# Narrow norms, an opening in blocks of tokens, and ada slabs moved into merge, in a fused two-block transformer kernel

## The chip, the cores and the metric

The kernel runs on 1 core of one Trainium2 chip. The metric is device time in microseconds (us); the time before is 2602.92 us, the median of 3 runs (2602.31 to 2603.13). The engines are PE (TensorE), DVE (VectorE), ACT (ScalarE), POOL (GpSimd) and SP (SyncE, which issues DMAs).

## The reference, cut to what matters

A block with three branches (forgetting attention, an S5 recurrence, attention over a memory) and a norm behind it, then two layers of a second block whose norms are modulated by a vector `c`:

```python
def rms(x, g):
    return x * rsqrt(mean(x * x, -1) + 1e-6) * g          # x: 512 tokens x 1024

def first_block(x, mem, ...):
    h = rms(x, g_norm)
    q, k, v, fl, gf, u, gs, qm, gm, gl = split_cols(h @ w_in)
    y_fox = forgetting_attention(q, k, v, log_sigmoid(fl + b_forget)) * silu(gf)
    y_s5 = ...     # s5_ssm(u, ...), gelu, glu with w_glu, * silu(gs)
    y_mem = ...    # attention to mem, * silu(gm)
    gates = sigmoid(gl + b_merge)                          # three gates of 1024
    merged = sum(gates[b] * (y[b] @ w_proj[b]) for b in range(3))
    return rms(x + merged @ w_out, g_final)

def second_block(x, c, ...):
    for l in range(2):
        sh1, sc1, gt1, sh2, sc2, gt2 = split(silu(c) @ w_ada[l] + b_ada[l], 6)
        h = rms(x, g_mix[l]) * (1 + sc1) + sh1
        mixed = ...    # h @ w_in_2[l], two attentions with rope and norms, gates
        x = x + gt1 * (mixed @ w_out_2[l])
        h2 = rms(x, g_mlp[l]) * (1 + sc2) + sh2
        x = x + gt2 * (square(relu(h2 @ w_ff1[l])) @ w_ff2[l])
    return x
```

All in float32.

## The kernel before, in words

**Layout.** x and h stand transposed in SBUF, as `xT` and `hT`: 8 tiles (k = 0 to 7) of 128 channels by 512 tokens. `hT` is a pair, a rounded high part (`hT_high`, type fp32r) and the rest (`hT_low`), and a product is three matmuls: high x high, low x high, high x low. A tile of output (128 columns of weights by 512 tokens) takes 8 x 3 = 24 matmuls (L433 in `tiles_stage`, L525 in `Stream`).

**Weights.** They come in slabs of 1 MB (256 columns by 1024 rows) through a ring of 3 slots (`SLOTS`). `plan_slabs` writes their order down; `load_weights` (SP) issues them in that order, and slab i waits until slab i-3 is given up (by the split, by a reduction or by PE). POOL splits a slab into a high and a low part in halves of 128 columns (L226, then L228), into 4 buffers for halves. The projections of merge (`w_proj_*`) are used without a split.

**Ada slabs.** `silu(c) @ w_ada` has one row only. Its 48 slabs stand between the others, one at a time: ACT scales a slab in place (L332, 8 operations), DVE reduces it (L345), PE adds over the partitions (L358, `ada_sum`), and DVE takes the result (L368, `ada_take`). In a stage these steps hang on the tiles: a slab whose last neighbour is tile n is handled from tile n-2 on. PE's sum of a slab waits until the last one was taken.

**A norm** (`rms_stage`). Squares on ACT (L612), sums over channels with a matrix of ones on PE (L627, the result on all partitions), a root on ACT (L614, 128x512), a reciprocal on DVE (L646, 128x512), and then per k: normed tile on DVE (L651), high part on ACT (L619), low part on DVE (L639 or L641). L631 are products without use that keep PE going. The first product that follows waits for each k (`arriving`): its tile takes one k at a time as `hT` arrives, and the next tile comes after it. With `summed` the squares were added up on DVE before (`add_square`, L584 and L585), behind each residual.

**The order of the stages.** `load_stage` loads the constants, x and small vectors, turns them on PE (L430) and copies them out on DVE. Then `s5_stages`: nine loads of parameters on ACT's queue (L997 to L1006), the first norm, the products u, gs, q and k, and in parallel a long DVE chain on the S5 parameters, which begins with their turn on PE (L1149) and has the sines on ACT (L1213, L1214) in its middle. `merge_stage` goes through four groups of columns (mp), in each three pairs (b) of a gate slab and a projection slab; a pair makes two tiles, 2 x (24 + 12) or 2 x (24 + 8) matmuls; ACT takes the gate (L1702), DVE multiplies and adds (L1708 to L1715). The last product of the first block, `out` (L433, taken by L1773), has four slabs with one ada slab each. Then come the norm `g_final` and, in `layer`, the gains (L1994, L1995), nine loads for rope and its gains on ACT's queue (L2000, L2006), the mixer's norm and qkv (L1858, tiles of 128 tokens by 256 columns). Behind attention: the residual (L2138), the mlp norm, and the mlp with relu (L2167) and the square (L2179 to L2181), where ada slabs stand again in layer 0.

## Time and profile before

| what | value |
|---|---|
| median of 3 runs | 2602.92 us |
| profiled execution | 2601.7 us, its span 2599.7 us |
| mean granted PE clock | 0.964 |
| PE busy | 2384.8 us, 92% of the span |
| DVE busy | 1454.2 us, 56% |
| POOL busy | 1126.4 us, 43% |
| ACT busy | 597.2 us, 23% |
| HBM read | 257.87 MB |

The span runs from the first to the last instruction of the profiled execution; all times of events are counted from its start. Busy time is the time with an instruction in execution. An instruction's bracket at the end of a row of the timeline, as [0.73 <-DVE normed L651], says how long the engine stood idle before it and which engine's work, which tile and line, ended that. Chain rows give the start, the duration, the engine and the line of a stretch on the chain that ended last, and the number of its instructions. The granted clock (PEclk) is a share of full speed, 1.00 for 2.4 GHz and 0.50 for 1.2 GHz.

### The profile page before, as it was taken

What the parts mean: (1) busy time and instruction counts of PE and PEld (TensorE: products, weight loads), DVE (VectorE), ACT (ScalarE), POOL (GpSimd) and SP (SyncE); (2) the same over time, 40 slices, a digit from 0 to 9 for tenths busy, and PEclk for the clock granted to TensorE, in tenths of its full rate; (3) what the DMA queues carried; (4) which work ended last, traced back from release to release, by engine and by line L of the source; (5) the groups of instructions that cost most, each with busy time, mean ns of one, the idle gap of its engine ahead of it and who ended that gap; (6) DMA issues with size and microseconds to landing.
All of it is one profiled execution on the core that took longest, in us unless ns stands there. A gap on an engine that the chain in (4) does not pass through costs nothing.

```text
span 2599.7 us, 30892 instructions
## 1 busy us (share of the span) xinstructions
PE 2384.8 (92%) x12709; PEld 1889.6 (73%) x12709; DVE 1454.2 (56%) x1756; ACT 597.2 (23%) x1212; POOL 1126.4 (43%) x672
## 2 busy tenths in 40 slices
PE   5798868799999969999998999998999999899998
PEld 3677835677666639977756888886997766688887
DVE  3799444424333667455458857747645537764341
ACT  2133325313222221134402334201114430100000
POOL 3543223143333525642124666663662305466663
PEclk8899978899999989999999999998999999999999
DMA  5334660341444432221032665533231104233321
GB/s 163 114 77 111 182 235 1 122 146 61 133 146 148 157 96 99 97 78 48 18 107 72 202 192 177 178 109 103 89 98 61 34 17 146 65 98 98 97 97 49
DMA packets 274280, 280.87 MB, mean 108 GB/s; under 512 B 29580, under 2 KB 256080, under 8 KB 274012
## 3 DMA queue, kind: packets, MB, share of 16 engines
q1 hardware_dynamic: 242012, 243.97, 29.6%
q10 hardware_dynamic: 32128, 34.92, 4.4%
q8 instruction: 101, 1.65, 0.3%
q14 instruction: 39, 0.32, 0.0%
HBM read 257.87 MB, written 17.85 MB: 106 GB/s over the span
## 4 chain that ended last, share of the span: by engine, by line
PE 68%; DVE 5%; ACT 1%; issue 1%; ACTq 0%; DVEq 0%
PE ps L433 43%; PE ps L1858 11%; PE ps L525 6%; PE ps L757 2%; PE ps L800 2%; PE ps L776 1%; DVE ps L864 1%; DVE normed L651 1%; DVE hT_low L641 1%; PE ps L786 1%; DVE root L646 1%; PE ps L627 1%; PE ps L1954 1%; PE ps L358 0%; DVE squares_summed L585 0%
## 5 line engine op out<-in xcount | busy, mean ns | idle before, releaser
L226 POOL TENSOR_SCALAR ring_high<-ring 128x1024 fp32r<-128x1024 f32 x302 | 335.1, 1110 | 1347.7 <-DMA ring<-in_w_in_dram 360.9
L228 POOL TENSOR_TENSOR ring_low<-ring,ring_high 128x1024 fp32r<-128x1024 f32 x302 | 762.2, 2524 | 25.2
L433 PE MATMUL ps<-hT_high,ring_high 128*128 128x512 f32 x816 | 329.1, 403 | 19.1 <-DVE hT_low L641 5.8
L433 PE MATMUL ps<-hT_low,ring_high 128*128 128x512 f32 x816 | 319.3, 391 | 0.0
L433 PE MATMUL ps<-hT_high,ring_low 128*128 128x512 f32 x816 | 319.2, 391 | 0.0
L345 DVE TENSOR_REDUCE ada_acc<-ring 128x256 f32<-128x2048 f32 x48 | 188.8, 3934 | 111.4 <-ACT ring L332 111.1
L1858 PE MATMUL ps<-ring_high,hT_high 128*128 128x256 f32 x768 | 221.8, 289 | 10.4 <-DVE hT_low L641 10.4
L1858 PE MATMUL ps<-ring_high,hT_low 128*128 128x256 f32 x768 | 219.6, 286 | 0.0
L1858 PE MATMUL ps<-ring_low,hT_high 128*128 128x256 f32 x768 | 219.5, 286 | 0.0
L332 ACT ACTIVATE ring<-ring,c_act 128x256 f32<-128x256 f32 x384 | 158.5, 498 | 186.2 <-DMA ring<-in_w_ada_dram 186.1
L433 PE MATMUL ps<-hidden_high,ring_high 128*128 128x512 f32 x512 | 200.0, 391 | 0.0
L525 PE MATMUL ps<-hT_high,ring_high 128*128 128x512 f32 x456 | 191.5, 420 | 9.2 <-ACT staged L1042 3.7
L433 PE MATMUL ps<-hidden_high,ring_low 128*128 128x512 f32 x512 | 199.3, 389 | 0.0
L433 PE MATMUL ps<-hidden_low,ring_high 128*128 128x512 f32 x512 | 199.2, 389 | 0.0
L433 PEld LDWEIGHTS ps<-hT_high,ring_high 128*128 128x128 f32 x816 | 154.3, 189 | 59.8 <-DVE hT_low L641 11.7
L525 PE MATMUL ps<-hT_low,ring_high 128*128 128x512 f32 x456 | 180.9, 397 | 0.0
L525 PE MATMUL ps<-hT_high,ring_low 128*128 128x512 f32 x456 | 180.8, 396 | 0.0
L433 PEld LDWEIGHTS ps<-hT_low,ring_high 128*128 128x128 f32 x816 | 154.3, 189 | 32.9 <-issue 2.9
L433 PEld LDWEIGHTS ps<-hT_high,ring_low 128*128 128x128 f32 x816 | 154.0, 189 | 32.6
L2138 DVE SCALAR_TENSOR_TENSOR xT<-ps,ada,xT 128x512 f32<-128x512 f32 x64 | 47.9, 750 | 220.9 <-PE ps L433 220.9
L1858 PEld LDWEIGHTS ps<-ring_high,hT_high 128*128 128x128 f32 x768 | 149.6, 195 | 14.7 <-DVE hT_low L641 11.1
L1858 PEld LDWEIGHTS ps<-ring_high,hT_low 128*128 128x128 f32 x768 | 149.9, 195 | 0.0
(341 smaller groups left out, 4164.1 us busy)
## 6 DMA issues: line engine op xcount, KB each, us to landing
ring<-in_w_in_dram SPq DMA_DIRECT2D x75, 1024.0 KB, 5.3
ring<-in_w_ff_dram SPq DMA_DIRECT2D x64, 1024.0 KB, 5.5
ring<-in_w_ada_dram SPq DMA_DIRECT2D x48, 1024.0 KB, 7.3
ring<-in_w_out_dram SPq DMA_DIRECT2D x12, 1024.0 KB, 6.6
scratch_x<-xT ACTq DMA_DIRECT2D x3, 2048.0 KB, 7.5
xT<-scratch_x ACTq DMA_DIRECT2D x3, 2048.0 KB, 8.6
ring<-in_w_mem_kv_dram SPq DMA_DIRECT2D x4, 1024.0 KB, 5.5
ring<-in_w_branch_a_dram SPq DMA_DIRECT2D x8, 512.0 KB, 6.1
```

Source lines behind the costliest of these rows:

```text
L226: nc.gpsimd.tensor_scalar(hi, raw, 1.0, 1.0, ALU.mult, ALU.mult).then_inc(hi_done.sem, 1)
L228: nc.gpsimd.tensor_tensor(lo, raw, hi.bitcast(F32), ALU.subtract).then_inc(lo_done.sem, 1)
L332: ins = K.nc.scalar.activation(w[:, k, :], w[:, k, :], ACT.Copy, scale=K.c_act[:, k:k + 1])
L345: K.nc.vector.tensor_reduce(K.ada_acc[:, n % 2, :], K.slot(slab).rearrange("p k n -> p n k"), AX_X, ALU.add).then_inc(K.sig("ada_scaled"). ...
L433: ins = nc.tensor.matmul(out[0:rows, bank, cols[0]:cols[1]], lhsT, rhs, start=start, stop=stop)
L525: ins = K.nc.tensor.matmul(out, lhsT, rhs, start=start, stop=stop)
L627: nc.tensor.matmul(K.ps[:, 0, 0:n], K.ones, K.sums[:, 0:n] if summed else sq[:, k % 2, 0:n], start=(k == 0), stop=(k == KS - 1)).then_inc( ...
L641: x = v.scalar_tensor_tensor(dst[1][:, k, 0:n], tmp[:, k % 2, 0:n], shift[:, k:k + 1], h, ALU.add, ALU.subtract)
L757: ins = nc.tensor.matmul(s_view(i, u, w)[:, c:c + n], lhsT, rhs, start=True, stop=st["diagonal"] is None or c + n < w)
L800: ins = nc.tensor.matmul(st["place"](o_view(j), u), st["values"](u, b), turned[j % T_BUFS][:, u, b * P:(b + 1) * P], start=(b == 0), stop= ...
L1858: ins = nc.tensor.matmul(out, lhsT, rhs, start=start, stop=stop)
L2138: return v.scalar_tensor_tensor(K.xT[:, m, :], ps[:, 0, :], gate[:, m:m + 1], K.xT[:, m, :], ALU.mult, ALU.add)
```

## The change

- **Opening** (`load_stage`). Slab 0 is loaded in front of x, and x in four blocks of 128 tokens, each with its own semaphore. ACT squares each block along its free axis with a sum of it (4 operations of 128x1024), one root and one reciprocal of 128x4 follow, and the rstd of the 512 tokens is put on all partitions by a product of ones with four diagonal matrices (128x512, `diag`). The transposes of x go block by block, the copies out of PSUM are shared by DVE and ACT, and the first norm is a part of this stage. The silu of `c` comes behind it. The S5 parameters are loaded by SP, in front of slab 3.
- **Norms** (`norm_stage`). The sums over channels are made narrow: each block of 128 tokens is the stationary side and a column of ones moves, so a sum is 128x1 and all four are 128x4. Root and reciprocal work on 128x4; the diagonals and one product spread the result. The last square is not added on DVE but summed by PE on its own. A small root in front loads ACT's table early. Behind `out`, one stage makes both norms (`twice`): from the sums of the squares of x and of x times `g_final` it has both factors, makes `hT` at once, and writes the normed `xT` afterwards. The squares behind `out` move from DVE to ACT (`out_squares`), the sums stay on DVE, one tile later.
- **First products.** Where a product waits for arriving tiles, its first two tiles (at qkv token tiles 0 and 2, then 1 and 3, of the first slab) are interleaved k by k.
- **Ada slabs.** Each of the four groups of merge has one more ada slab, behind the first gate slab; `out` has none.
- **Rope loads.** Those of layer 0 are issued ahead of `out`, those of layer 1 behind the mlp norm of layer 0.

```diff
+        if i == 0:
+            continue
...
             add(f"merge{mp}{b}g", w, dm, O_GL + D * b, D, part=mp)
+            if b == 0:
+                ada(0)
             add(f"merge{mp}{b}p", T[pw][0], (0, rows), 0, D, False, part=mp)
             ada(0)
-    add_ada("out", T["w_out"][0], dm, 0, D, 0)
+    add("out", T["w_out"][0], dm, 0, D)
...
+            if arriving is not None:
+                first = 2
+                size = len(tiles[0])
+                per = 1 if tiles[0][0][5][1] is None else 3
+                for j in range(0, size, per):
+                    pe.wait_ge(arriving[0].sem, arriving[1] + max(j // per + 1, arriving[3]))
+                    for n in range(2):
+                        for x in range(j, j + per):
+                            ins = product(n, x)
+                        if j + per == size:
+                            ins.then_inc(made.sem, 1)
...
+            if self.arriving is not None and n < 2:
+                k, x = divmod(self.fed, 6)
+                n, j = x // 3, 3 * k + x % 3
+                if x == 0:
+                    pe.wait_ge(self.arriving[0].sem, self.arriving[1] + k + 1)
...
+    if n == 0:
         return K.nc.vector.tensor_tensor(K.sums, x, x, ALU.mult)
-    K.link(e, "dve_step", K.nc.vector.tensor_tensor(sq, x, x, ALU.mult))
+    ins = K.nc.vector.tensor_tensor(sq, x, x, ALU.mult)
+    if n == KD - 1:
+        return ins
+    K.link(e, "dve_step", ins)
     return K.nc.vector.tensor_tensor(K.sums, K.sums, sq, ALU.add)
 
...
+def norm_stage(K, src, gain, dst, shift, sums, last, twice=None):
...
+            nc.scalar.activation(nar[:, 6, 0:1], K.eps[:, 0:1], ACT.Sqrt)
...
+            def turn(bank, x, last):
+                for t in range(TT):
+                    ins = nc.tensor.matmul(ps[:, bank + t, 0:1], x[:, t * P:(t + 1) * P], K.ones[:, 0:1],
+                                           start=not last, stop=last)
+                return ins
...
+            if twice is not None:
+                squared, summed = twice[0]
+                pe.wait_ge(tiles.sem, tiles.total - 1)
+                pe.wait_ge(summed.sem, summed.total)
+                turn(2, twice[3], False)
+                warm(2)
+                pe.wait_ge(squared.sem, squared.total - 1)
+                turn(2, twice[4], True).then_inc(turned.sem, 1)
+                for t in range(TT):
+                    x = slice(t * P, (t + 1) * P)
+                    nc.tensor.matmul(ps[:, 6, t:t + 1], sums[:, x], K.ones[:, 0:1], start=True, stop=False)
+                    if t == 0:
+                        pe.wait_ge(squared.sem, squared.total)
+                    ins = nc.tensor.matmul(ps[:, 6, t:t + 1], last[:, x], K.ones[:, 0:1], start=False, stop=True)
+                ins.then_inc(turned.sem, 1)
+                pe.wait_ge(tiles.sem, tiles.total)
+                warm(2)
+            else:
+                pe.wait_ge(tiles.sem, tiles.total - 1)
+                turn(2, sums, False)
+                warm(1)
+                pe.wait_ge(tiles.sem, tiles.total)
+                turn(2, last, True).then_inc(turned.sem, 1)
+                warm(1)
+            pe.wait_ge(diagonal.sem, d0 + 1)
+            nc.tensor.matmul(ps[:, 7, :], K.ones, diag[:, 0], start=True, stop=True).then_inc(spread.sem, 1)
+            if twice is not None:
+                nc.tensor.matmul(ps[:, 6, :], K.ones, diag[:, 1], start=True, stop=True).then_inc(spread.sem, 1)
+                warm(1)
+            else:
+                warm(3)
+        @block.scalar
+        def _(e):
+            if twice is not None:
+                e.wait_ge(turned.sem, t0 + 1)
+                nc.scalar.activation(nar[:, 0, :], ps[:, 2:6, 0], ACT.Sqrt, bias=K.eps[:, 0:1], scale=1.0 / D
+                                     ).then_inc(root.sem, 1)
+                e.wait_ge(scaled.sem, s0 + 1)
+                nc.scalar.activation(nar[:, 3, :], nar[:, 2, :], ACT.Sqrt, bias=K.eps[:, 0:1], scale=1.0 / D
+                                     ).then_inc(root.sem, 1)
+            else:
+                e.wait_ge(turned.sem, t0 + 1)
+                nc.scalar.activation(nar[:, 3, :], ps[:, 2:6, 0], ACT.Sqrt, bias=K.eps[:, 0:1], scale=1.0 / D
+                                     ).then_inc(root.sem, 1)
...
+        @block.vector
+        def _(e):
+            step = lambda ins: K.link(e, "dve_step", ins)
+            def diagonals(j, x):
+                return v.tensor_tensor(diag[:, j], K.ident.unsqueeze(1).broadcast_to([P, TT, P]),
+                                       x.unsqueeze(2).broadcast_to([P, TT, P]), ALU.mult)
+            n = 0
+            e.wait_ge(root.sem, o0 + 1)
+            if twice is not None:
+                step(v.reciprocal(nar[:, 1, :], nar[:, 0, :]))
+                e.wait_ge(turned.sem, t0 + 2)
+                step(v.tensor_tensor(nar[:, 2, :], ps[:, 6, 0:TT], nar[:, 1, :], ALU.mult))
+                v.tensor_tensor(nar[:, 2, :], nar[:, 2, :], nar[:, 1, :], ALU.mult).then_inc(scaled.sem, 1)
+                diagonals(1, nar[:, 1, :])
+                e.wait_ge(root.sem, o0 + 2)
+                step(v.reciprocal(nar[:, 4, :], nar[:, 3, :]))
+                step(v.tensor_tensor(nar[:, 4, :], nar[:, 4, :], nar[:, 1, :], ALU.mult))
+                n = 1
+            else:
+                step(v.reciprocal(nar[:, 4, :], nar[:, 3, :]))
+            diagonals(0, nar[:, 4, :]).then_inc(diagonal.sem, 1)
+            def low_part(k):
+                e.wait_ge(high.sem, h0 + k + 1)
+                v.scalar_tensor_tensor(dst[1][:, k, :], tmp[:, k % 2, :], shift[:, k:k + 1], dst[0][:, k, :].bitcast(F32),
+                                       ALU.add, ALU.subtract).then_inc(low.sem, 1)
+            e.wait_ge(spread.sem, w0 + 1)
...
+    def load_parameters(sp):
...
+        sp.wait_ge(K.sig("x_turned").sem, KD)
+        sp.wait_ge(K.sig("x_squared").sem, TT)
+        sp.dma_start(lamn[:, 0, 0:P5], T["lam_re"][0]).then_inc(loaded.sem, 16)
...
+    K.sync_turns[K.first["u"] + SLOTS] = [load_parameters]
...
+            sp.dma_start(K.const[:, :], T["const_main"]).then_inc(cl.sem, 16)
+            sp.dma_start(K.slot(0), K.slabs[0][0][0]).then_inc(K.sig("slab_landed0").sem, 16)
+            for t in range(TT):
+                sp.dma_start(xn[:, t, :], T["x"][0, t * P:(t + 1) * P, :]).then_inc(xl[t].sem, 16)
...
+            pe.wait_ge(cl.sem, 16)
+            for t in range(TT):
+                pe.wait_ge(xl[t].sem, 16)
+                for n in range(KD):
+                    ins = nc.tensor.transpose(ps[:, n, t * P:(t + 1) * P], xn[:, t, n * P:(n + 1) * P], K.ident)
+                    if t == TT - 1:
+                        ins.then_inc(turned.sem, 1)
+            pe.wait_ge(ld.sem, 16 * (2 + len(vec)))
...
+            pe.wait_ge(diagonal.sem, 1)
+            nc.tensor.matmul(ps[:, 1, :], K.ones, diag[:, :, :], start=True, stop=True).then_inc(spread.sem, 1)
+            pe.wait_ge(by_dve.sem, 3)
+            for _ in range(3):
+                nc.tensor.matmul(ps[:, 2, 0:3 * P], K.ident, K.const[:, 0:3 * P], start=True, stop=True)
+        @block.scalar
+        def _(e):
+            e.wait_ge(eps.sem, 1)
+            nc.scalar.activation(nar[:, 6, 0:1], K.eps[:, 0:1], ACT.Sqrt)
+            for t in range(TT):
+                e.wait_ge(xl[t].sem, 16)
+                if t:
+                    e.wait_ge(squared.sem, t)
+                nc.scalar.activation(squares[:, :], xn[:, t, :], ACT.Square, accum_out=nar[:, 0, t:t + 1]
+                                     ).then_inc(squared.sem, 1)
+            e.wait_ge(squared.sem, TT)
+            nc.scalar.activation(nar[:, 3, :], nar[:, 0, :], ACT.Sqrt, bias=K.eps[:, 0:1], scale=1.0 / D
+                                 ).then_inc(root.sem, 1)
...
+            evict(0)
+            evict(1)
+            e.wait_ge(root.sem, 1)
+            K.link(e, "dve_step", v.reciprocal(nar[:, 4, :], nar[:, 3, :]))
+            v.tensor_tensor(diag[:, :, :], K.ident.unsqueeze(1).broadcast_to([P, TT, P]),
+                            nar[:, 4, :].unsqueeze(2).broadcast_to([P, TT, P]), ALU.mult).then_inc(diagonal.sem, 1)
+            evict(2)
+            evict(3)
+            e.wait_ge(by_dve.sem, 4)
+            e.wait_ge(cols.sem, 1)
+            e.wait_ge(spread.sem, 1)
...
+    rope_loads(K, T, 0)
...
+        if 2 <= n:
+            e.wait_ge(squared.sem, 2 * n)
+            for x in range(2):
+                a = square[:, 0, x, :] if n == 2 else sums[x]
+                ins = v.tensor_tensor(sums[x], a, square[:, (n - 1) % 2, x, :], ALU.add)
+            ins.then_inc(summed.sem, 1)
...
+    def out_squares(e, n):
+        e.wait_ge(added.sem, added0 + n + 1)
+        if n >= 2:
+            e.wait_ge(summed.sem, n - 1)
+        nc.scalar.activation(square[:, n % 2, 0, :], xq[:, n, :], ACT.Square).then_inc(squared.sem, 1)
+        nc.scalar.activation(square[:, n % 2, 1, :], xq[:, n, :], ACT.Square, scale=K.g_final[:, n:n + 1]
+                             ).then_inc(squared.sem, 1)
...
+                    order = [(t + u, 3 * k + x) for u in range(2) for k in range(KD) for t in (0, 2) for x in range(3)]
...
+            if l == 0:
+                K.link(e, "gains_ready", v.tensor_scalar(gains[:, 2, :], ada[:, 16:24], 0.5, None, ALU.mult))
+                v.tensor_tensor(gains[:, 3, :], gains[:, 0, :], K.g_final, ALU.mult).then_inc(ga.sem, 1)
+            else:
+                v.tensor_scalar(gains[:, 2, :], ada[:, 16:24], 0.5, None, ALU.mult).then_inc(ga.sem, 1)
...
+        arriving = norm_stage(K, xq, gains[:, 3, :], K.hT, ada[:, 0:8], sums[1], last[1],
+                              (squared, K.g_final, K.xT, sums[0], last[0]))
+    else:
+        K.close(gains=ga)
+        arriving = norm_stage(K, K.xT, gains[:, 0, :], K.hT, ada[:, 0:8], K.sums, K.square_last)
...
-    arriving = rms_stage(K, K.xT, SEQ, gains[:, 1, :], K.hT, shift=ada[:, 24:32], summed=True)
+    arriving = norm_stage(K, K.xT, gains[:, 1, :], K.hT, ada[:, 24:32], K.sums, K.square_last)
+    if l + 1 < LAYERS:
+        rope_loads(K, T, l + 1)
```

SP's loads in the second group of merge, before (`ring<-in_w_in` is a gate slab, `ring<-in_w_ada` an ada slab, in brackets what the slot waits for):

```order
L202 DMA ring<-in_w_in_dram 128x8x256 [waits half_split]
L202 DMA ring<-in_w_proj_fox_dram 128x6x256 [waits tile_made]
L202 DMA ring<-in_w_ada_dram 128x8x256 [waits ada_scaled]
L202 DMA ring<-in_w_in_dram 128x8x256 [waits half_split]
L202 DMA ring<-in_w_proj_s_dram 128x6x256 [waits tile_made]
```

and now:

```order
L204 DMA ring<-in_w_in_dram 128x8x256 [waits half_split]
L204 DMA ring<-in_w_ada_dram 128x8x256 [waits tile_made]
L204 DMA ring<-in_w_proj_fox_dram 128x6x256 [waits ada_scaled]
L204 DMA ring<-in_w_ada_dram 128x8x256 [waits half_split]
L204 DMA ring<-in_w_in_dram 128x8x256 [waits ada_scaled]
L204 DMA ring<-in_w_proj_s_dram 128x6x256 [waits tile_made]
```

An ada slab stands between the gate slab and the first projection slab, and the next gate slab waits for an ada slab's slot instead of a split.

ACT at the mlp norm of layer 0, before:

```order
L614 ACT_TABLE_LOAD [waits x_back,square_used,tile_made]
L614 ACTIVATE root_9849<-ps,eps 128x512 [waits tile_taken]
L619 ACTIVATE hT_high<-normed_9850,ada 128x512 [waits norm_scaled] x8
L79 UNCONDITIONAL_BRANCH
L2167 ACTIVATE relu_9928<-ps 128x512 [waits norm_high,tile_made,square_used,norm_low]
L332 ACTIVATE ring<-ring,c_act 128x256 [waits slab_landed2]
```

and now:

```order
L718 ACT_TABLE_LOAD
L718 ACTIVATE narrow<-eps 128x1
L79 UNCONDITIONAL_BRANCH
L778 ACTIVATE narrow<-ps,eps 128x4 [waits x_back,sums_turned,tile_taken,tile_made]
L784 ACTIVATE hT_high<-normed_9831,ada 128x512 [waits norm_scaled] x8
L79 UNCONDITIONAL_BRANCH
L2281 DMA rope_9916<-in_const_rope_dram 128x1024 [waits norm_low,norm_high,rstd_spread]
L2287 DMA gn_9917<-in_q_norm_a_dram 128x64
L2287 DMA gn_9917<-in_k_norm_a_dram 128x64
```

The table is loaded without a wait, root and sum are 128x4, and the nine loads for layer 1's rope (three of them shown) stand between the last high part and the first relu.

ACT in the opening, before, from the silu of `c` to the first squares:

```order
L1564 ACTIVATE c_act<-cols 128x8 [waits inputs_loaded]
L79 UNCONDITIONAL_BRANCH
L997 DMA lamn<-in_lam_re_dram 48x64 [waits c_activated,biases_halved]
L998 DMA lamn<-in_lam_re_dram 48x64
L999 DMA lamn<-in_lam_im_dram 48x64
```

and now, its first operations:

```order
L1749 ACT_TABLE_LOAD
L1749 ACTIVATE narrow<-eps 128x1 [waits eps_set]
L1754 ACTIVATE x_squares,narrow<-xn 128x1024 [waits x_loaded0]
L1754 ACTIVATE x_squares,narrow<-xn 128x1024 [waits x_squared,x_loaded1]
L1754 ACTIVATE x_squares,narrow<-xn 128x1024 [waits x_squared,x_loaded2]
L1754 ACTIVATE x_squares,narrow<-xn 128x1024 [waits x_squared,x_loaded3]
L1757 ACTIVATE narrow<-narrow,eps 128x4 [waits x_squared]
```

The squares wait for a block of x each and for nothing else; the loads of the parameters have left ACT's queue.

## Rows read from the trace of the kernel before

**Rows 1.** The page, part 4: chain that ended last, by engine.

```profile
PE 68%; DVE 5%; ACT 1%; issue 1%; ACTq 0%; DVEq 0%
```

**Rows 2.** Windows of the opening: busy time (count) by engine, PEclk, DMA share, GB/s.

```profile
7.00:8.00 1.00, 0.00 (x0) 0.00 (x0) 0.00 (x0) 0.00 (x0) 0.00 (x0) 1.00 1.03 401
```

**Rows 3.** Timeline of PE, opening: start us, us, line, operation, count [idle before <-releaser].

```profile
10.93 0.59 PE L430 MATMUL ps<-const,rows 100*128 100x100 f32 x2 [10.93 <-DMA b_forget_col<-in_b_forget_dram]
61.37 0.39 PE L1149 MATMUL ps<-const,lamn 48*128 48x48 f32 x3
```

**Rows 4.** Timeline, opening: POOL, then DVE.

```profile
17.84 2.36 POOL L228 TENSOR_TENSOR ring_low<-ring,ring_high 128x1024 fp32r<-128x1024 f32 x1
...
40.33 3.35 DVE L646 RECIPROCAL root<-root 128x512 f32<-128x512 f32 x1 [20.09 <-ACT root L614]
43.71 1.42 DVE L651 SCALAR_TENSOR_TENSOR normed<-xT,cols,root 128x512 f32<-128x512 f32 x2
```

**Rows 5.** Timeline of ACT, the sines of the S5 coefficients.

```profile
109.40 1.28 ACT L1213 ACT_TABLE_LOAD   x1
```

**Rows 6.** Merge: page part 6; ACT and DVE timelines; chain row of PE.

```profile
ring<-in_w_in_dram SPq DMA_DIRECT2D x75, 1024.0 KB, 5.3
...
651.21 0.69 ACT L1702 ACTIVATE merge_tmp<-ps,half_b_merge 128x512 f32<-128x512 f32 x1 [6.67 <-PE ps L433]
...
698.78 3.30 ACT L332 ACTIVATE ring<-ring,c_act 128x256 f32<-128x256 f32 x8 [6.95 <-DMA ring<-in_w_ada_dram]
...
644.57 3.79 DVE L345 TENSOR_REDUCE ada_acc<-ring 128x256 f32<-128x2048 f32 x1 [2.41 <-ACT ring L332]
...
714.27 0.15 DVE L368 TENSOR_TENSOR ada<-ps,cols 128x2 f32<-128x2 f32 x1
...
691.44 21.40 PE ps L433 x72
```

**Rows 7.** `out` and the norms behind it: chain rows, timelines, one window.

```profile
879.86 18.25 PE ps L433 x72
...
926.86 0.50 PE L358 MATMUL ps<-const,ada_acc 128*128 128x1 f32 x4
...
930.87 2.65 POOL L228 TENSOR_TENSOR ring_low<-ring,ring_high 128x1024 fp32r<-128x1024 f32 x1
...
917.51 0.69 DVE L585 TENSOR_TENSOR squares_summed<-squares_summed,square 128x512 f32<-128x512 f32 x1
...
962.49 1.41 DVE L651 SCALAR_TENSOR_TENSOR normed<-xT,gains,root 128x512 f32<-128x512 f32 x2
...
973.54 137.81 PE ps L1858 x1134
...
970.00:980.00 10.00, 8.48 (x47) 7.73 (x48) 9.77 (x32) 2.12 (x3) 0.00 (x0) 0.67 0.48 178
```

**Rows 8.** Mlp norm of layer 0: timelines; L627 by its source (ns, min/median/max); chain row.

```profile
947.71 0.45 ACTq L2006 DMA_DIRECT2D gn<-in_k_norm_b_dram  x1
...
1393.22 2.65 POOL L228 TENSOR_TENSOR ring_low<-ring,ring_high 128x1024 fp32r<-128x1024 f32 x1
...
1393.71 2.71 DVE L585 TENSOR_TENSOR squares_summed<-squares_summed,squared 128x512 f32<-128x512 f32 x1
...
L627 PE MATMUL ps<-squares_summed,const x8: 667/1061/1221, 931.5 to 2223.8; 128*128 128x512 f32 x8
...
1404.15 1.42 DVE L651 SCALAR_TENSOR_TENSOR normed<-xT,gains,root 128x512 f32<-128x512 f32 x2
...
1417.16 0.60 ACT L2167 ACTIVATE relu<-ps 128x512 f32<-128x512 f32 x1 [1.92 <-PE ps L433]
...
1435.84 11.02 PE ps L433 x48
```

**Rows 9.** Timeline of DVE, mixer norm of layer 1.

```profile
1777.52 0.24 DVE L1994 SCALAR_TENSOR_TENSOR gains<-ada,cols 128x8 f32<-128x8 f32 x2
...
1786.10 1.41 DVE L651 SCALAR_TENSOR_TENSOR normed<-xT,gains,root 128x512 f32<-128x512 f32 x2
```

More of the change, by code:

```diff
@@ L397, in tiles_stage @@
             ada.setdefault(max(n - 2, 0), []).append(K.ada_after[key])
+    for slabs in ada.values():
+        slabs.sort()
     if ada and dve is None:
@@ L438, in _ @@
                 ada_sum(K, pe, s)
-        if act is None and ada:
+        if act is None and (ada or also is not None):
             @block.scalar
@@ L443, in _ @@
                 for n in range(N):
+                    if also is not None:
+                        also(e, n)
                     for s in ada.get(n, []):
@@ L656, in _ @@
                 low_part(KD - 1)
[L658 to L659 removed]
+    ready.total += KD
+    used.total += KD
     root.total += 1
@@ L1503, in load_stage @@
     rows = R("rows", [P, 2, P], 24576)
-    ld = K.sig("inputs_loaded")
+    squares = R("x_squares", [P, D], 28672)
+    diag = R("diagonals0", [P, TT, P], 49152)
+    tmp = R("normed0", [P, 2, SEQ], 57344)
+    nar, dst = K.narrow, K.hT
+    ld, cl = K.sig("inputs_loaded"), K.sig("const_loaded")
+    xl = [K.sig(f"x_loaded{t}") for t in range(TT)]
     vec = [("g_norm", 8), ("g_mem_norm", 8), ("g_final", 8), ("b_merge", 24), ("s5_d", 6), ("b_glu", 6),
@@ L1553, in load_stage @@
+    ld.total += 16 * (2 + len(vec))
+    cl.total += 16
+    for g in (*xl, ):
+        g.total += 16
+    for g in (eps, root, diagonal, spread, rows_turned, cols):
+        g.total += 1
+    for g in (squared, by_dve, by_act):
+        g.total += 4
+    for g in (turned, scaled, high, low):
+        g.total += KD
+    K.close(loads=ld, tensor=spread, xdve=by_dve, xact=by_act, cols=cols)
+    arriving = (low, 0, dict(K.last), 1)
+    K.close(scalar=high, vector=low)
     ha, si = K.sig("biases_halved"), K.sig("c_activated")
@@ L2006, in _, with layer @@
                 e.dma_start(gn[:, i, :], a.broadcast_to([P, HD])).then_inc(rl.sem, 16)
-    ga.total += 1
-    K.close(vector=ga)
-    arriving = rms_stage(K, K.xT, SEQ, gains[:, 0, :], K.hT, shift=ada[:, 0:8], summed=l > 0)
+def layer(K, T, l):
+    nc, R = K.nc, K.region
+    v = nc.vector
+    gains = K.gains
+    ada = K.ada[:, l, :]
+    ga = K.sig("gains_ready")
+    rope, gn = K.rope
+    with K.stage() as block:
+        @block.vector
+        def _(e):
+            for i, (at, g) in enumerate(((8, K.g_mix[l]), (32, K.g_mlp[l]))):
+                v.scalar_tensor_tensor(gains[:, i, :], ada[:, at:at + 8], 1.0, g, ALU.add, ALU.mult)
+            if l == 0:
[3 more added lines that the diff above has]
+                v.tensor_scalar(gains[:, 2, :], ada[:, 16:24], 0.5, None, ALU.mult).then_inc(ga.sem, 1)
+    ga.total += 1
+    if l == 0:
+        K.close(vector=ga)
+        xq, squared, sums, last = K.outer
+        arriving = norm_stage(K, xq, gains[:, 3, :], K.hT, ada[:, 0:8], sums[1], last[1],
[3 more added lines that the diff above has]
+        arriving = norm_stage(K, K.xT, gains[:, 0, :], K.hT, ada[:, 0:8], K.sums, K.square_last)
     sx, xs = K.scratch_x.rearrange("(t p) n -> p t n", p=P), K.sig("x_spilled")
```

294 lines of the change are left out of this document (180 added, 114 removed).

## The prediction

> **What bounds the kernel now.** I read the chain that ended last first: TensorE (PE) holds 68% of it and VectorE 5% [rows 1]. PE is busy 92% of the span, so a cheaper operation elsewhere is worth nothing unless PE waits for it. The views by time come next, since such an average hides the places where PE stands. There are five: the opening; the change of norm after `out`; and the norm ahead of the mlp or the mixer three times more. The opening's first product of `hT` can't start before VectorE's L651 at 43.71 [rows 4], and the next piece of work, L1149, starts at 61.37 [rows 3]. After the last product of `out` (with its sums, 927.36) the first L651 of the mixer's norm is at 962.49 [rows 7], 35.1 us later. Last come the two stages into which the removed ada slabs move: the four groups of merge, where PE runs without a gap [rows 6], so that whatever arrives late there is paid in full.
>
> **The opening.** Before, nothing is computed until the last small vector has landed at 10.93 [rows 3], the squares stand on ScalarE (ACT) behind nine parameter DMAs, and a wide root and a wide reciprocal (3.35 us [rows 4]) follow. After, x comes in four blocks, each squared at once. DMA moves 401 GB/s in the window in which x ends [rows 2], so the 1 MB slab in front costs x 2.6 us at that rate; I take 3, since not every window reaches it, so the last block lands near 11.8 and the vectors near 13.9. Last square 12.9, narrow root 13.2, narrow reciprocal and diagonals (0.24 and 0.75 us by their nearest operations) 14.3; the vectors' transposes stand ahead of the spread on PE, so it runs 14.6 to 16; the copies out of PSUM end at 15.9. First normed tile 16.0 to 17.5; I take 16.8. From there to L1149 it was 17.66 us, of which 24 matmuls of 0.227 (5.45) were the second tile; it is now interleaved, so 6 matmuls (1.38) ride on each 1.39 us step, with 0.7 left at the end: 12.9. Slab 1 is split by POOL from about 16 to 23, and each of its L228 (2.36 [rows 4]) can hold a low-part subtraction that reads two SBUF tiles: two of them, 3.7. End: 33.4 instead of 61.4, 28.0 gained. The parameters, now on SP behind x, land by 31 at the latest, just in time. The VectorE chain of the S5 coefficients starts at L1149 and runs unbroken to the sines; there a table load of 1.28 stood in front of them [rows 5], and the order no longer has one: 1.3. **Opening: 29** (bounds 20, if the clock, the parameters or a slow first block eat 9; 32, if no subtraction meets a split).
>
> **Merge.** It takes four more ada slabs. First, in group 0 the gate slab of branch 1 must wait for the ring slot of an ada slab, free when its reduction ends at 648.36 [rows 6]: 5.3 us to land and 3.5 for its first half's split give 657.2, where its tile was due at 651.2: the wait is about 5.7. Second, in the three later groups the projection slab now stands behind an ada slab on SP. Before, it was the ada slab that stood behind, and it was there at 698.78, 7.34 behind the group's first product at 691.44 [rows 6]; the projection's products come 24 x 0.227 = 5.45 behind it: 1.9 each, 5.7. (The Trainium skill, DMA: Bandwidth & Descriptors, Queues, rings and completion order, has the descriptors of one queue start in order; a reader may say that they overlap and the projection lands sooner. By the rule the wait is 1.9; by free overlap it is 0.) Third, two ada sums now stand behind one another, and the second waits for the first to be taken: from the tile's end at 712.84 to the take's end at 714.42 plus a hand-over, 1.75, three times, and 2.6 at the tile with two VectorE operations: 7.85. **Merge: -19.3** (0 if none of the three arises; -25 if each wait also lets the clock fall). **`out`** loses its four sums with their gaps, 0.5 each [rows 7]: **+2.1**.
>
> **Norm after `out`.** The first norm of all of x and the second are one now. Count from PE's end: the residual 1.2, two squares on ACT 1.3, narrow turns on PE (a 128x1 product of fp32 with its loads costs what the four of L358 show, 0.5 for two) 2 to 2.3, two narrow roots, two reciprocals and three products some 2, the diagonals 0.75, the spread 1.35 (two passes of 0.667 at full clock, 1.2 each at the worst [rows 8]). That is 8.8; POOL splits until about 6 us behind PE's end [rows 7], which can hold the first diagonals, so I take 10.5 for the first normed tile, against 35.1: 24.6. The first qkv slab then interleaves two token tiles: 24 matmuls of 0.12 (137.81 over 1134 [rows 7]) go under the steps, 2.8; and the half-clock stretch behind the norm (granted 0.67 over 970 to 980 [rows 7]) is entered with less to do: 2.2. **24.6 + 5.0 = 29.6.** Bounds 22 (wide, blocked by POOL) and 31.
>
> **Mlp norm, layer 0.** The chain was square, sum, one wide product, table, wide root, wide reciprocal. The sum (2.71 under POOL's 2.65 [rows 8], 0.69 without it [rows 7]) and the wide steps go; what is left of it that reads two SBUF tiles is the diagonals, and they wait for POOL to end at 1395.87. Then 0.75, spread 1.35, hand-overs 0.25: first normed at 1398.2 instead of 1404.15. (The Trainium skill, GPSIMD Engine Reference, Specifications, says that GpSimd and VectorE contend where VectorE has two SBUF inputs; the trace agrees, 2.71 against 0.69. By the rule the diagonals wait for the split, without it they would start at 1395.) The last low part is at 1410.1. But nine rope DMAs are now queued on ACT ahead of the first relu: 9 x 0.48 = 4.3 [rows 8], so the relu is at 1414.45, not 1411.5; it was 1417.16, 2.7 later. Behind the relu hangs a fixed chain to tile 4: ada scale, reduction, slab load, split, 18.7 us (1417.16 to 1435.84 [rows 8]). PE sits idle through 10 us of it and starts again at the lower clock; the restart in `out` cost 1.9 (18.25 for 72 products that take 16.35 at 0.227 [rows 7]). **+1** (bounds -2 and 9, if the chain let tile 4 start as early as the norm).
>
> **Mixer norm, layer 1.** POOL's split holds the gains until 1777.5 [rows 9]; gains 0.4, reciprocal 0.24, diagonals 0.75, spread 1.35: 1780.0 against 1786.10, 6.1. Its half-clock stretch is the longer one, interleave and clock together 6.2. **+12.3** (8 to 14). **Mlp norm, layer 1.** As layer 0 to its first normed tile, 5.95 earlier, but with no rope DMA and no ada behind it. The second tile's 5.45 goes under the steps and 0.6 of it comes back at the end, 4.85: **+10.8** (6 to 11).
>
> **Sum.** 29 - 19.3 + 2.1 + 29.6 + 1 + 12.3 + 10.8 = 65.5. The profiled execution took 2601.7 us (span 2599.7), 1.2 below the median 2602.92; 2601.7 - 65.5 = 2536.2, and as a median about **2537**.
>
> **Rivals.** *The merge costs don't arise*: the projection and ada land side by side, or the gate's slab gets its slot early. For it, the DMA engines are idle ahead of each group; against it, 7.34 for the same bytes. All 19.3 come back: 2518. *The opening keeps only 20*: the parameters arrive late, or the clock falls in the wait behind the spread. For it, VectorE's chain, which ends the S5 coefficients, also waits for DMA; against it, SP can issue them from about 13.5 on, and that chain asks for them 20 us later. The 9 are lost: 2546. *The lock*: the narrow operations meet POOL or the lower clock in all four norms, the diagonals' 2.65 twice and a spread of 2.4; 3 each, 12 in all: 2549. For it, 2.71 on the sums of both layers; against it, one split is over in 2.7 and POOL has nothing more to do until tile 0 is through. *The other side, slower*: PE now stands between many short products and falls to its lower clock (window 970 to 980 was 0.67) and stays there through qkv. Each of its 1134 matmuls would cost 0.12 more; the change's gain is gone from some 540 matmuls on, and one whole stage gives 2537 + 138 = 2675. Against it, the 1134 matmuls behind the norm of before took 0.12 on average, though the first of them ran in that state.
>
> **How the numbers follow.** Forecast 0.55, merge for nothing 0.13, opening 20 0.13, the lock 0.15, slower 0.03, and 0.01 that the edits cancel. A change of 0.2%, 5 us, is what a measurement of this kernel can tell. All but the last two end below 2597: faster 0.96, same 0.01, slower 0.03. The range 2514 to 2562 holds the forecast with the bounds of its terms and the first three rivals' centres; the tails of these, the slower case and sums of two rivals leave some 2 in 10 out.
>
> **What would show it.** In the profile after: the first normed tile near 16.8 and L1149's place near 33.4; PE waiting for a projection slab in three merge groups and for the gate's split in the first; `out` without sums; the first normed tile behind `out` at PE's end + 10.5; relu of layer 0 behind the rope DMAs and PE idle before tile 4; and the product after each norm two tiles wide. I am wrong if the time is above 2562, most likely through the clock, or below 2514, if merge hides its slabs.

## The result, and the profile after

The changed kernel takes 2572.8 us (median of 4 runs, 2570.01 to 2575.04), the kernel before in the same and the earlier runs 2602.61 (2593.82 to 2603.13). The ratio is 0.9884, 95% interval 0.987 to 0.9897: some 30 us faster, where 65 were forecast. The profiled execution has a span of 2572.3 us against 2599.7, so 27.4 us are to be found in the traces.

| stretch (its end, before and after) | forecast | measured | with the placement mended (e1) |
|---|---|---|---|
| opening, to merge's first product (627.72, 600.26) | 29 | 27.5 | 29.3 |
| merge (876.12, 882.17) | -19.3 | -33.5 | -31.5 |
| `out` (927.36, 932.48) | 2.1 | 0.9 | 2.2 |
| norm behind `out` and qkv (1111.35, 1092.94) | 29.6 | 23.5 | 21.5 |
| attention and `out` of layer 0 (1392.04, 1374.78) | 0 | -1.1 | -1.3 |
| mlp norm and mlp, layer 0 (1773.10, 1759.71) | 1 | -3.9 | 2.8 |
| mixer norm to `out`, layer 1 (2218.32, 2196.20) | 12.3 | 8.7 | 10.1 |
| mlp norm to the end, layer 1 | 10.8 | 5.3 | 10.4 |
| sum | 65.5 | 27.4 | 43.5 |

The last column is the profiled execution of the first experiment.

**The opening** answers to [rows 3, 4]. From the timeline after, PE, VectorE and POOL (start, duration, line, operation, in brackets the idle time before and what ended it):

```profile
15.51 1.10 PE L1741 MATMUL ps<-diagonals,const 128*128 128x512 f32 x2 [0.37 <-DVE diagonals L1782]
33.94 0.38 PE L1329 MATMUL ps<-const,lamn 48*128 48x48 f32 x3
...
14.66 0.69 DVE L1782 TENSOR_TENSOR diagonals<-const,narrow 128x512 f32<-128x512 f32 x1
16.75 1.41 DVE L1800 SCALAR_TENSOR_TENSOR normed<-xT,cols,ps 128x512 f32<-128x512 f32 x2 [0.20 <-PE ps L1741]
18.20 2.83 DVE L1792 TENSOR_TENSOR hT_low<-normed,hT_high 128x512 fp32r<-128x512 f32 x1
23.17 2.08 DVE L1792 TENSOR_TENSOR hT_low<-normed,hT_high 128x512 fp32r<-128x512 f32 x1
...
18.13 2.34 POOL L230 TENSOR_TENSOR ring_low<-ring,ring_high 128x1024 fp32r<-128x1024 f32 x1
22.01 2.69 POOL L230 TENSOR_TENSOR ring_low<-ring,ring_high 128x1024 fp32r<-128x1024 f32 x1
```

The first normed tile comes at 16.75 (forecast 16.8) and the turn of the S5 parameters, L1329, at 33.94 (forecast 33.4, before 61.37), 27.4 us earlier. Of the eight low parts two ran under POOL's split, 2.83 and 2.08 instead of 0.68, as reckoned.

**Merge**, chain after, first group, the second group's first tiles (start, duration, engine, line, number):

```profile
600.26 13.52 PE ps L431 x36
614.57 3.21 ACT ring L336 x8
617.80 3.79 DVE ada_acc L349
621.61 5.35 DMA ring<-in_w_in_dram
628.16 2.35 POOL ring_low L230
630.55 13.75 PE ps L431 x36
...
650.88 12.14 PE ps L431 x36
663.36 17.91 PE ps L431 x64
681.70 7.21 DMA ring<-in_w_proj_fox_dram
688.95 16.07 PE ps L431 x48
...
707.31 22.98 PE ps L431 x72
```

and what PE waited for in merge (in total, times, longest):

```profile
PE ps L362 <- DVE ada L372: 9.4, 4, 5.3
PE ps L431 <- POOL ring_low L230: 6.1, 1, 6.1
PE ps L431 <- DMA ring<-in_w_proj_fox_dram: 6.0, 3, 2.5
```

The mechanisms are those of the forecast. In the first group the second gate slab is loaded when the ada slab is reduced (621.61), lands and is split, and PE waits 6.1 us (5.7 forecast). In each later group PE waits for the projection slab, 6.0 in three. The sums of ada waited 9.4 (7.85 forecast), of which 5.3 in the first group where 2.6 was put down: there VectorE reduces the next ada slab ahead of the tile's two operations and the take:

```profile
644.74 3.62 DVE L349 TENSOR_REDUCE ada_acc<-ring 128x256 f32<-128x2048 f32 x1 [18.82 <-PE ps L362]
```

So PE stands 21.6 us in merge, where it stood for nothing before, and the forecast had 19.3. The other 12 us of the 33.5 are not waits. The mean granted clock of the stage is 0.95 instead of 0.99: after, beside a stretch at the start that both have, it is 0.50 for 10.2 us from 626.4, for 6.8 from 646.9 and for 3.4 from 708.4 and from 776.6. So 36 products take 13.75 and 12.14 us in the first group and 72 take 22.98 and 22.99 in the second and third, where 72 took 21.40 before, 10.7 for 36 [rows 6]: 7.7 us. The 48 products right behind the projection slab lose nothing: 24 of them are the projection's (429 ns each, before and after), and 21.40 less 24 x 0.227 is 15.95, against 16.07. The four more sums take 0.6 to 1.0 each, 2.7. (The Trainium skill, DMA: Bandwidth & Descriptors, Queues, rings and completion order, has descriptors of one queue start in order; the trace agrees: ada slab, projection slab and ada slab, issued at 681.28, 681.70 and 682.33, land in this order at 686.66, 688.90 and 691.81.)

**The norm behind `out`** [rows 7], after:

```profile
932.51 2.13 DVE L2046 TENSOR_TENSOR squares_summed<-squares_summed,square 128x512 f32<-128x512 f32 x2 [2.49 <-PE ps L431]
934.57 1.08 DVE L2049 SCALAR_TENSOR_TENSOR x_by_residue<-ps,xT 128x512 f32<-128x512 f32 x1
943.54 0.69 DVE L798 TENSOR_TENSOR diagonals<-const,narrow 128x512 f32<-128x512 f32 x1
946.67 1.41 DVE L826 SCALAR_TENSOR_TENSOR normed<-x_by_residue,gains,ps 128x512 f32<-128x512 f32 x2 [2.43 <-PE ps L760]
...
937.05 1.69 PE L727 MATMUL ps<-const,square 128*128 128x1 f32 x8
938.60 0.56 PE L745 MATMUL ps<-const,squares_summed 128*128 128x1 f32 x2
939.03 0.57 PE L748 MATMUL ps<-const,square 128*128 128x1 f32 x2
944.71 1.91 PE L760 MATMUL ps<-diagonals,const 128*128 128x512 f32 x2
```

PE's last product ends at 932.48; the first normed tile follows after 14.2 us, not 10.5 (before 35.1). The last residual (L2049) stands behind two sums (L2046, 2.13; POOL splits beside them, until 936.87). The twelve narrow products behind the squares (L727 four; L745 and L748 four each, of which one pair of each is shown; two passes a product) take 5.1 us from 937.05, where 2 to 2.3 was forecast: the granted clock is 0.50 from 937.0 to 947.2. POOL's split was over when the diagonals came, and they took 0.69.

That it is the clock, a second execution of the same norm shows. In the profiled one of e12 below, the clock stayed at 1.00 until the products were done:

```profile
937.57 0.95 PE L727 MATMUL ps<-const,square 128*128 128x1 f32 x8
938.38 0.36 PE L745 MATMUL ps<-const,squares_summed 128*128 128x1 f32 x2
...
939.94 0.36 PE L748 MATMUL ps<-const,square 128*128 128x1 f32 x2
```

The twelve take 2.7 us there, from 937.57 to 940.30, and the first normed tile comes 11.6 us behind the last product of `out`. In e1, e7 and e9 the clock fell earlier, 2 to 3 us behind that product; there the products without use in front of the narrow ones ran at the lower clock too and held them up, and the tile came after 16.1 to 16.3. So this norm varies by 4.7 us between executions of the same instructions, with the moment at which the clock falls; what sets that moment no run shows.

**The mlps.** The chain rows of the last one, before and after:

```profile
2241.48 344.59 PE ps L433 x1518
```

```profile
2204.35 353.97 PE ps L431 x1536
```

344.59 over 1518 is 227.0 ns a product, 353.97 over 1536 is 230.4. PE waits for nothing in either and its granted clock is 1.00 in both. That was in no part of the forecast. Product by product, in the stages at full clock, the gap from one start to the next is 226.8 ns before everywhere in the mlp; after, it is 226.8 where `hT` is the moving operand and 233.3 where `hidden` is, and the same 233.3 in the three `out` products (`merged`, `mixed`).

### The profile page after: what moved, and what is told of

The parts are those of the page before. It is cut to its first block, busy times and chain, and to the rows that moved or that the text cites. A ratio compares the mean times of both kernels' runs of the same rounds, so it can differ in the third digit from the quotient of the medians.

```text
span 2572.3 us, 30947 instructions
## 1 busy us (share of the span) xinstructions
PE 2382.6 (93%) x12717; PEld 1890.9 (74%) x12717; DVE 1422.9 (55%) x1754; ACT 600.9 (23%) x1231; POOL 1133.7 (44%) x672
## 4 chain that ended last, share of the span: by engine, by line
PE 68%; DVE 4%; ACT 1%; DMA 1%; issue 1%; POOL 1%; ACTq 0%; DVEq 0%; SPq 0%; POOLq 0%
PE ps L431 44%; PE ps L2148 10%; PE ps L552 6%; PE ps L940 2%; PE ps L983 2%; PE ps L959 1%; DVE ps L1047 1%; DMA ring<-in_w_proj_fox_dram 1%; PE ps L969 1%; DVE normed L826 1%; DVE hT_low L819 1%; PE ps L2244 1%; PE ps L362 0%; DVE ada_acc L349 0%; ACT probs_b L1002 0%
## 5 line engine op out<-in xcount | busy, mean ns | idle before, releaser
L228 POOL TENSOR_SCALAR ring_high<-ring 128x1024 fp32r<-128x1024 f32 x302 | 344.2, 1140 | 1310.8 <-DMA ring<-in_w_in_dram 382.2
L431 PE MATMUL ps<-hT_high,ring_low 128*128 128x512 f32 x816 | 323.7, 397 | 0.0
L431 PE MATMUL ps<-hT_low,ring_high 128*128 128x512 f32 x816 | 323.6, 397 | 0.0
L552 PE MATMUL ps<-hT_high,ring_low 128*128 128x512 f32 x456 | 182.4, 400 | 0.0
L552 PE MATMUL ps<-hT_low,ring_high 128*128 128x512 f32 x456 | 182.4, 400 | 0.0
```

Of the source, the lines that this page charges most:

```text
L228: nc.gpsimd.tensor_scalar(hi, raw, 1.0, 1.0, ALU.mult, ALU.mult).then_inc(hi_done.sem, 1)
L431: return nc.tensor.matmul(out[0:rows, bank, cols[0]:cols[1]], lhsT, rhs, start=start, stop=stop)
L552: ins = K.nc.tensor.matmul(out, lhsT, rhs, start=start, stop=stop)
```

## The experiments

**e1 to e3, e12: where the operands lie.** The change makes `gains` larger (by 32 bytes a partition) and adds `narrow` (112 bytes, which take 128, since each tensor starts at a multiple of 32). These small tensors stand in front of `xT`, `hT` and the ring, which thereby move by 160 bytes and start 32 bytes off a multiple of 64, while the regions (`hidden`, `merged`, `mixed`) are rounded up to one. e1 puts them back:

```diff
+    K.pad = nc.alloc_sbuf_tensor("pad", [P, 8], F32)
     K.rowsum = nc.alloc_sbuf_tensor("rowsum", [P, 4, 2], F32)
```

> The changed kernel with 32 more bytes per partition allocated in front of xT, so that xT, hT and the weight ring start at a multiple of 64 bytes, as they do in the kernel before; in the changed one they start 32 bytes off, while hidden and merged start at a multiple of 64. Theory A (where the operands of a product lie sets its pace): the 512-wide products of out and of the second half of the mlp, at 233.3 ns each in the changed kernel and 226.7 in the one before, are all at 226.7 again; some 2100 of them by 6.67 ns is 14 us, so 2558 to 2560. Theory B (the pace belongs to the execution or to the instruction stream): 2572 as before, and the blocks of 233.3 ns stay.

Measured 2557.07 us (2551.18 to 2566.07), ratio to before 0.9824 (0.9801 to 0.9848). Chain row of the last mlp:

```profile
2193.48 348.77 PE ps L431 x1536
```

348.77 over 1536: 227.1 ns. Theory A holds. e2 is the kernel before with the same line:

> The kernel before with the same 32 bytes, which here move xT, hT and the ring 32 bytes off a multiple of 64 and leave hidden and merged on one. Theory A: slower by some 14 us (2603 to 2617) with blocks of 233.3 ns in the products of hidden and merged. Theory B: the time of before within 2 us.

Measured 2615.1 us against 2603.12, ratio 1.0046 (1.0029 to 1.0063), so 12 us slower, 14 forecast; 233.3 ns in all products of `hidden`, `mixed` and `merged`. e3 leaves out the rounding, so that both operands are 32 bytes off:

```diff
-    base = (nc.sbuf_base + 63) // 64 * 64
+    base = nc.sbuf_base
```

> The changed kernel with xT, hT and ring 32 bytes off as it has them, and the regions (hidden, merged, normed and others) not rounded up to 64 bytes, so that these lie 32 bytes off too. Theory A1 (what counts is that the moving and the stationary operand lie alike): all products at 226.7, 2558 to 2560. Theory A2 (what counts is each operand alone against 64 bytes): nothing is gained, 2572, or more if the elementwise work suffers too.

Measured 2558.76 us, ratio 0.9827 (0.9812 to 0.9841): as good as e1. e12 is e1 with the regions moved:

```diff
-    base = (nc.sbuf_base + 63) // 64 * 64
+    base = (nc.sbuf_base + 63) // 64 * 64 + 32
```

> The aligned kernel with xT, hT and ring at a multiple of 64 bytes and the regions (hidden, merged and the others) 32 bytes off, the mirror of the changed kernel. Theory A1 (moving and stationary operand must lie alike): products of hidden and merged at 233.3 ns again, 12 to 16 us slower than the aligned kernel. Theory A2 (it is the stationary operand's 32 bytes that cost, and only where hT does not lie the same way): stays at 226.7 and at the aligned time.

Measured 2573.48 us in one run. The last mlp of e3 and of e12:

```profile
2194.12 348.74 PE ps L431 x1536
```

```profile
2203.52 353.98 PE ps L431 x1536
```

With the kernel before, these are all four combinations, and the two where both lie alike are the fast ones. So neither operand's own place sets the pace but the difference of the two: 226.8 ns where moving and stationary operand lie alike against 64 bytes, 233.3 where they differ by 32. 2112 products (192 of `merged`, 384 of `mixed`, 1536 of `hidden`) times 6.5 ns are 13.7 us, and the medians differ by 15.7 between e1 and the changed kernel, whose runs (2551 to 2566, 2570 to 2575) leave room for that. Only offsets of 0 and 32 bytes were run.

**e4: the ada slabs of merge back in `out`.**

```diff
-            if b == 0:
-                ada(0)
...
-    add("out", T["w_out"][0], dm, 0, D)
+    add_ada("out", T["w_out"][0], dm, 0, D, 0)
```

> The aligned kernel with the four ada slabs of merge back in out, as before. If merge lost 33 us by them (from the traces: its first group 17.6 longer, the next three 5.6, 6.3 and 3.6) and out gained 1, this is 30 us faster than the aligned kernel, less what of the 33 was the slower pace: 2528 to 2534. If the loss in merge has another cause (the shifted opening, the pace), it is within 5 us of the aligned one.

Measured 2547.46 us (ratio 0.9782, 0.9766 to 0.9799), 10 below e1 instead of 30. Merge was right: 598.52 to 844.95, 246.4 us, against 248.4 before and 279.9 in e1. The gain went to `out`, whose chain now reads:

```profile
857.88 0.61 ACT square L2057
858.49 3.21 ACT ring L334 x8
...
865.48 1.06 DVE x_by_residue L2047
866.56 0.63 ACT square L2056
867.19 0.61 ACT square L2057
867.80 3.20 ACT ring L334 x8
...
874.71 3.85 DVE squares_summed L2044 x2
```

The squares are on ACT now. A slab's scaling (3.21) stands between them, VectorE's sums wait for them and the next residual for the sums: 57.0 us from the first product to the last where e1 needs 45.3. With the norm and qkv it is 229.5 us from merge's end to the end of qkv, against 211.5 in e1: the slabs cost 18 there. My expectation left this out: the squares' move and the slabs' move belong together.

**e7: the four last slabs of layer 0 in its own mlp.** Their result, columns 40 to 47, is first used by the residual of that mlp.

```diff
-            if b == 0:
-                ada(0)
...
+        after_start = 0
...
                 if l + 1 < LAYERS:
-                    ada(l + 1)
+                    if after_start >= 2:
+                        ada(l if n_ada[l] < 24 else l + 1)
+                    after_start += 1
...
-        rope_loads(K, T, l + 1)
+        rope_by_sync(K, T, l + 1)
```

> The aligned kernel with three edits: no extra ada slab in merge; none in out either, the last four slabs of layer 0 (whose result is first used by the second half of layer 0's mlp) go into that mlp with the 24 of layer 1, and none of them stands behind the first two slabs of the mlp; the rope loads of layer 1 are issued by SP in the middle of the mlp instead of by ACT ahead of its first relu. If merge's loss is all due to the extra slabs (35 us between the aligned kernel and the one with them in out), if out is bound by ada's scaling ahead of the squares (18 us between the same two), and if PE's idle 10 us ahead of the mlp's fifth tile are those of the ada chain: 2557 - 35 - 10 = 2512, 2505 to 2520. If the ada slabs cost the same wherever they stand: 2545 to 2557.

Measured 2515.15 us (2511.96 to 2515.37), ratio 0.9655 (0.9633 to 0.9677): the fastest version, 3.4% below the kernel before, and inside the expected range. PE has no wait at all in merge, and the first group's three tiles are whole again:

```profile
596.02 33.76 PE ps L432 x108
```

**e8 and e5: what holds the mlp's fifth tile.** e8 is e1 with only the `after_start` lines of above, e5 is e1 with only `rope_by_sync`, which issues the nine loads on SP in the middle of the mlp.

```diff
+    K.sync_turns.setdefault(K.first[f"ff1{l - 1}20"], []).append(turn)
```

> The aligned kernel with the 24 ada slabs of layer 1's modulation starting behind the third slab of layer 0's mlp instead of the first; merge and the rope loads as in the changed kernel. Theory: the chain relu, ada scale, reduction, load, split sets when PE starts its fifth tile; without it PE goes on, the idle 10 us and the restart at the lower clock go: 2557 - 10 = 2547, 2544 to 2550. Rival: the same chain only comes two slabs later, and the time stays within 2 us of 2557.

> The aligned kernel with the nine rope loads of layer 1 on SP's queue in the middle of the mlp, not on ACT's ahead of the first relu. Theory: the relu comes 4.3 us earlier and the chain behind it with it: 2553, 2551 to 2555. Rival: VectorE or the slab's load, not the relu, sets the fifth tile: 2557 within 1.

e8: 2549.8 us (0.9794, 0.977 to 0.9818), 7.3 below e1; from the last product of `out` to the last of the mlp 372.1 us against 378.3. Its chain has no ada in front of the fifth tile:

```profile
1379.06 27.81 PE ps L434 x120
```

e5: 2556.25 us, 0.8 below e1, inside the spread. Chains of e1 and e5 at the fifth tile:

```profile
1412.02 0.58 PE ps L362 x4
1412.60 11.02 PE ps L431 x48
1423.95 11.04 PE ps L431 x48
```

```profile
1405.90 0.58 PE ps L362 x4
1406.48 12.63 PE ps L431 x48
1419.45 11.04 PE ps L431 x48
```

The relu came 3.3 us earlier and the fifth tile with it, 37.5 us behind the last product of `out` instead of 40.7, so the rival's reason is wrong. But its pair of tiles then took 12.63, at the lower clock, where e1's took 11.02: half of the 3.2 was given back there. The changed kernel, with the loads on ACT, has 12.62 at this place, so the edit is not shown to be the cause of that. The time is the rival's all the same: the edit alone gains nothing that these runs can tell.

**e9: merge's extra slab in three groups only.**

```diff
-            if b == 0:
+            if b == 0 and mp > 0:
                 ada(0)
```

> The aligned kernel with the extra ada slab in merge's groups 1 to 3 only; the fourth goes into layer 0's mlp (last slab of layer 0, 25 slabs in that stage from its first tile on). Theory: the first group of merge, 17 us longer in the aligned kernel because its second gate slab waits for the slot of an ada slab whose reduction comes late, is as long as before (63.7), and groups 1 to 3 stay 4 to 6 us longer each: merge 15 to 18 us shorter than in the aligned kernel. Rival: the first group's loss moves into the second, whose first pair is then the first with an extra slab: merge 5 us shorter at most.

Measured 2543.95 us in one run. Merge took 263.0 us from its first product to its last, 279.9 in e1: 16.9 shorter. The first group:

```profile
600.43 33.76 PE ps L434 x108
```

108 products in 33.76 us, as before (34.10). The rival falls.

**e10: the first tiles one after the other.**

```diff
-                for j in range(0, size, per):
-                    pe.wait_ge(arriving[0].sem, arriving[1] + max(j // per + 1, arriving[3]))
-                    for n in range(2):
+                for n in range(2):
+                    for j in range(0, size, per):
+                        if n == 0:
+                            pe.wait_ge(arriving[0].sem, arriving[1] + max(j // per + 1, arriving[3]))
...
-                    order = [(t + u, 3 * k + x) for u in range(2) for k in range(KD) for t in (0, 2) for x in range(3)]
+                    order = order
```

> The aligned kernel with the first two tiles behind each norm one after the other again. By the sum of the forecast it loses 4.8 behind the last mlp norm, 2.8 each at the two qkv stages, 5 in the opening, nothing ahead of layer 0's mlp (the ada chain hides it): 15, 2572 in all. Rival: PE stands at its lower clock there anyway and the second tile costs more, up to twice: 2585.

Measured 2577.05 us in one run, its span 18.8 above e1's, of which 5.6 up to merge, 1.2 in merge, 4.3 behind the last mlp norm, 4.0 in layer 1 up to its last `out`, 3.9 in layer 0's qkv, 2.6 in layer 0's mlp. The norm behind `out` took 3 less, which is no work of the edit: the clock fell later than in e1 and was back at 1.00 for the narrow products, which began 6.1 us behind the last product of `out` and took 2.9 us. e3, which interleaves, has the same 15.7 us from the last product of `out` to the first of qkv, where e1 has 18.7. More than the 15 forecast, less than the rival.

**e11: the opening of before** (`load_stage`, the parameters on ACT's queue, `rms_stage`) in e1.

```diff
-        block_one(K, T, load_stage(K, T))
+        load_stage(K, T)
+        block_one(K, T)
...
-    K.sync_turns[K.first["u"] + SLOTS] = [load_parameters]
+    arriving = rms_stage(K, K.xT, SEQ, K.g_norm, K.hT)
```

> The aligned kernel with the opening of before (x in one load, slab 0 behind it, wide root and reciprocal, parameters on ACT's queue), but its first two tiles still interleaved. Theory: the new opening gives 27.5 us, of which the interleave's 5 stay: 2557 + 22.5 = 2579.5, 2576 to 2583. Rival: what the opening gains is given back behind it (merge's first group was 17.6 us longer in the changed kernel): 2557 to 2568.

Measured 2580.06 us (0.9907, 0.9882 to 0.9933), 23 above e1. Merge begins at 625.87 instead of 598.43, and the span is 24.5 longer: of 27.4 us at most 3 are given back behind the opening, where the rival asked for 16 and more. The median is that of the theory; that merge begins 27.4 us later and not 22.5 is in part a later first normed tile (45.23, 43.71 before) and 1.8 us of the varying part told below.

## Why the prediction was wrong

It was right on the direction and on most mechanisms, and 36 us too low (2537 against 2572.8). By its steps:

- *Opening: 29*, measured 27.5 and 29.3 up to merge, with the varying part below in between; L1149's place itself came 27.4 us earlier, for 28.0. Right, down to the two low parts under POOL's split. The rival that it keeps only 20 is out.
- *Merge: -19.3*, the mis-sized term. The three waits came about and nearly in their size, 21.6 us (6.1, 6.0 in three groups, 9.4 for the sums) for 19.3. But I priced only the waits. The lower clock behind them, 7.7 us, I had at nothing in the sum and only in the outer bound of -25, though the profile of before showed a restart's 1.9 in `out`; and the four sums' own 2.7 I left out. The first group was the dearest: its sum waited 5.3 and not 2.6, it holds 4.5 of the 7.7, and e9 gets 16.9 back by leaving out its extra slab alone, where I had 8.3. Some 1.5 us of the 33.5 stay unassigned.
- *`out`: 2.1*, measured 0.9 and, with the placement mended, 2.2. Right.
- *Norm behind `out`: 29.6*, measured 23.5. Two steps of the chain failed. The narrow turns took 5.1 us for 2 to 2.3, because PE ran them at its lower clock (2.7 at the full one in e12; by the 0.5 for two that the forecast cites, the twelve come to 3.0). And the residual stood 2.1 us behind VectorE's sums, which the count from PE's end did not have. What interleave and clock were to give in qkv, 5.0, came to 2.6. POOL's hold, for which I had added 1.7, did not come.
- *Mlp norm, layer 0: 1*, with e1 2.8. The fixed chain from relu to the fifth tile is there (1396.59 to 1414.86, 18.3 us), but PE stood idle in it for 6.6 us (4.3 and 2.4), not 10; e8 shows that the stage costs 6 us more than need be.
- *Layer 1: 12.3 and 10.8*, with e1 10.1 and 10.4. Right.
- *Nowhere*: the largest miss, the pace of products whose operands lie 32 bytes apart, 13.7 us by the count above, 15.7 by the medians. The sum put the allocation at nothing without a word. No row of before could show the cost, but the diff did show a tensor that grows and one that is new in front of all the large ones.

The sum of the misses in the profiled executions, 65.5 - 27.4 = 38.1: 16.1 is the placement (43.5 of e1 less 27.4), 12.2 merge, 8.1 the norm behind `out`, 2.2 and 0.4 the norms of layer 1, 1.3 attention, less 1.8, 0.3 and 0.1 gained elsewhere. Of the rival *the lock* (2549) the lower clock came in the norm behind `out` and, for 0.9 us, in layer 1's mixer norm (first normed tile 7.7 us behind PE's end, 6.7 in e8, where the clock stayed at 1.00; 6.9 forecast). In the two mlp norms the tile came after 5.7 us, where 6.2 was forecast. *The merge costs don't arise* is out, and *the other side* did not occur. No rival held the placement.

Left open: the attention and S5 part, which no edit touches. From the turn of the S5 parameters to merge it took 565.4 to 568.5 us in eleven of the profiled executions, 561.8 in e7 and 556.3 in e2, and why is not shown. So e2's profiled execution (2605.76) is the shortest of its four runs, and a single run's time can be off by as much; e9, e10 and e12 rest on their stretches.

## What to carry to other kernels

Ahead of any small tensor that is added or grown, look at the addresses behind it: here 144 bytes of new tensors took 16 of the 43 us that the edits gain, and one line of padding gave them back. A wait of PE is priced with what the lower clock costs behind it, not alone: here 7.7 us behind 21.6 of waits. And work that fills gaps is moved by where its result is first needed: four slabs that cost 32 us in merge, and 18 in `out` once the squares stood on ACT, cost nothing that the profile shows in the mlp that uses them (372.7 us in e7 with them and with the rope loads on SP, 372.1 in e8 without).

## What the hardware showed

A 128x512 product of fp32r takes 226.8 ns from start to start where moving and stationary operand lie alike against 64 bytes (both on a multiple, or both 32 off) and 233.3 where they differ by 32, at the same granted clock of 1.00: alike in before, e1 and e3, apart in the changed kernel, e2 and e12. A product with a narrow moving side (128x1, fp32, two passes with a load of the stationary side each) took 0.43 us at the granted clock of 0.50 (changed kernel) and 0.22 at 1.00 (e12).
